# Two hybrid layers and two attention layers on one core: probabilities turned by 32 x 32 blocks, scores as three fp32r products

## The reference, cut to what matters

```python
h = x @ w_in                                   # q, k, v, z for 12 heads of kind a and 12 of kind b, and gates
out_a = dilated_mixture(rope(qa), rope(ka), va)      # with 256 tokens: softmax(q.k/sqrt(128) + log count) @ v
out_b = forgetting_attention(qb, kb, vb, log_f)      # softmax(q.k/sqrt(128) + D_t - D_s), causal, @ v
```

## Time and profile before

| | |
|---|---|
| median of 3 runs | 2801.43 us (2800.37 to 2801.75) |
| the profiled execution | 2799.75 us, its span 2798.0 us |
| TensorE matmul busy | 2757.6 us, 99% |
| VectorE busy | 1817.0 us, 65% |
| ScalarE busy | 1346.3 us, 48% |
| GpSimd busy | 370.9 us, 13% |
| TensorE's granted clock | 0.994 of full |

### The profile page before, as it was taken

How to read it: one execution, slowest core, us unless ns; L and a number is a source line. 1 busy time by engine, 2 the same in 40 slices (tenths; PEclk the granted TensorE clock), 3 DMA queues, 4 the chain that set the end, 5 groups by cost and what they waited for, 6 DMA issues and landing times.

```text
span 2798.0 us, 35964 instructions
## 1 busy us (share of the span) xinstructions
PE 2757.6 (99%) x13157; PEld 2253.2 (81%) x13157; DVE 1817.0 (65%) x2220; ACT 1346.3 (48%) x1765; POOL 370.9 (13%) x653
## 2 busy tenths in 40 slices
PE   8899999999999999999999999999999999999998
PEld 5477887888888888888888888888888888888886
DVE  7889899778657556655555556575565545555565
ACT  3255646556544453544444544444445444445443
POOL 0000010000001223100133100022131011331000
PEclk9999999999999999999999999999999999999999
DMA  9987798865655566566566566565566665665554
GB/s 397 414 311 241 272 342 307 309 222 190 215 194 181 188 201 205 185 220 196 191 202 203 191 196 223 181 195 187 191 203 205 208 199 183 206 206 187 193 213 148
DMA packets 178617, 622.74 MB, mean 223 GB/s; under 512 B 27688, under 2 KB 27984, under 8 KB 173088
## 3 DMA queue, kind: packets, MB, share of 16 engines
q1 hardware_dynamic: 155376, 583.08, 60.3%
q0 software_dynamic: 23088, 37.56, 4.6%
HBM read 599.51 MB, written 2.14 MB: 215 GB/s over the span
## 4 chain that ended last, share of the span: by engine, by line
PE 90%; DMA 4%; DVE 4%; ACT 1%; issue 0%; SPq 0%; DVEq 0%; ACTq 0%
PE acc L860 65%; PE acc L2455 16%; DMA raw<-in_w 2%; DVE wlo L1865 1%; PE psS L839 1%; PE psS L829 1%; DMA scr<-in_w_early 1%; PE psS L2455 1%; PE psS L2421 1%; PE psT L812 1%; PE psT L2378 1%; DMA mraw<-in_w_early 1%; DVE raw L1900 0%; PE psS L2440 0%; PE psT L2340 0%
## 5 line engine op out<-in xcount | busy, mean ns | idle before, releaser
L489 DVE TENSOR_TENSOR wlo<-raw,whi 128x1024 fp32r<-128x1024 f32 x670 | 819.4, 1224 | 783.7 <-ACT whi L372 782.0
L372 ACT ACTIVATE whi<-raw 128x1024 fp32r<-128x1024 f32 x670 | 708.9, 1059 | 980.3 <-PE acc L860 964.4
L860 PE MATMUL acc<-whi,tokens_hi 128*128 128x512 f32 x2304 | 632.3, 395 | 0.5 <-DVE tokens_lo L303 0.3
L860 PE MATMUL acc<-whi,tokens_lo 128*128 128x512 f32 x2304 | 618.2, 389 | 0.0
L860 PE MATMUL acc<-wlo,tokens_hi 128*128 128x512 f32 x2304 | 618.1, 389 | 0.0
L860 PEld LDWEIGHTS acc<-whi,tokens_lo 128*128 128x128 f32 x2304 | 432.4, 188 | 91.5
L860 PEld LDWEIGHTS acc<-wlo,tokens_hi 128*128 128x128 f32 x2304 | 432.4, 188 | 91.0
L860 PEld LDWEIGHTS acc<-whi,tokens_hi 128*128 128x128 f32 x2304 | 425.7, 188 | 85.6 <-DVE tokens_lo L303 0.9
L1564 ACT ACTIVATE whi<-raw 128x1024 fp32r<-128x1024 f32 x160 | 168.7, 1058 | 200.8 <-PE acc L2455 116.2
L1865 DVE TENSOR_TENSOR wlo<-raw,whi 128x1024 fp32r<-128x1024 f32 x160 | 195.3, 1223 | 82.2 <-ACT whi L1564 81.3
L2455 PE MATMUL acc<-whi,tokens_hi 128*128 128x512 f32 x800 | 226.1, 403 | 1.9 <-DVE tokens_lo L1974 1.2
(11 more groups left out here) (355 smaller groups left out, 2434.2 us busy)
## 6 DMA issues: line engine op xcount, KB each, us to landing
raw<-in_w SPq DMA_DIRECT2D x838, 512.0 KB, 4.2
raw<-in_w_late SPq DMA_DIRECT2D x80, 512.0 KB, 5.0
mraw<-in_w SPq DMA_DIRECT2D x64, 512.0 KB, 4.7
mraw<-in_w_late SPq DMA_DIRECT2D x48, 512.0 KB, 4.8
y<-in_w_early SPq DMA_DIRECT2D x12, 1024.0 KB, 15.4
mraw<-in_w_early SPq DMA_DIRECT2D x7, 1024.0 KB, 14.9
scr<-in_w_early SPq DMA_DIRECT2D x7, 1024.0 KB, 14.8
sgl<-in_w_early SPq DMA_DIRECT2D x6, 1024.0 KB, 15.0
```

What stands on the lines that cost most here:

```text
L372: act.activation(whi[:, n % SLOTS, :], raw[:, n % SLOTS, :], ACT.Copy).then_inc(s_hi, 1)
L489: dve.tensor_tensor(wlo[:, n % SLOTS, :], raw[:, n % SLOTS, :], whi[:, n % SLOTS, :].bitcast(F32), ALU.subtract).then_inc(s_lo, 1)
L860: m = pe.matmul(acc[c % 2][:, tb, :], a[:, kk, tb * P:(tb + 1) * P], b[:, n % SLOTS, k * CW:(k + 1) * CW], start=(kk == 0 and q == 0), sto ...
```

## The change

The probabilities no longer pass through TensorE and ScalarE. At r = 35 VectorE turns all three units at once in 32 x 32 blocks into `pb`, which lies in the memory of `qT` and `kT`, and GpSimd moves the blocks to `probT` with 16 transfers of 32 partitions x 12 runs of 32 numbers. The scores become three fp32r products each (`qhi` `khi`, `qlo` `khi`, `qhi` `klo`), all three units in one place at r = 27; the halves are made by ScalarE and VectorE at their steps 27 (q) and 28 (k) and share memory with `stage`, `blocks` and `qkT`. Score unit 2 uses a `psT` bank as a fill. Both value units stand at r = 38. The turned heads move from r = 42 to r = 44. GpSimd's order becomes qT, kT, probT, zT.

```diff
-R_SCORES = 26
-R_BLOCKS = R_SCORES + 16
+R_SCORES = 27
+R_PROB = R_SCORES + 8
+R_BLOCKS = R_SCORES + 17
@@ fills2
-        if 0 <= r - R_SCORES - 5 <= 2:
-            out += [("p", grp, r - R_SCORES - 5)]
+        if r == R_SCORES:
+            out += [("s", grp, 2)]
@@ units2
-        if 0 <= r - R_SCORES <= 2:
-            out += [("s", grp, r - R_SCORES)]
-        if 0 <= r - R_SCORES - 10 <= 1:
-            out += [("o", grp, r - R_SCORES - 10)]
+        if r == R_SCORES:
+            out += [("s", grp, 0), ("s", grp, 1)]
+        if r == R_SCORES + 11:
+            out += [("o", grp, 0), ("o", grp, 1)]
@@ memory
+    stage, qhi = shared("stage", [P, TB, CW], "qhi", [P, HPG, SEQ])
+    qkT, qklo = shared("qkT", [P, 2 * HPG, SEQ], "qklo", [P, 2 * HPG, SEQ])
+    pb = qkT[:].rearrange("p h t -> p (h t)")[:, 0:3 * CW]
+    blocks, khi = shared("blocks", [P, TB, CW], "khi", [P, HPG, SEQ])
@@ gpsimd, regrouped
-                pool.wait_ge(s_blk, 3 * n + i + 1)
-                if grp:
-                    pool.wait_ge(*unit_full(l, ("s", grp - 1, 2)))
+                pool.wait_ge(s_blk, 4 * n + i + 1)
+                if n:
+                    pool.wait_ge(s_pT, MOVED * n)
...
-            pool.wait_ge(s_blk, 3 * n + 3)
+            pool.wait_ge(s_blk, 4 * n + 3)
             if n:
                 pool.wait_ge(s_alo, n)
+            blocks_moved(probT[:].rearrange("p u (k t) -> p (u k) t", t=P), pb.rearrange("p (k t) -> p k t", t=P), s_pT)
+            pool.wait_ge(s_blk, 4 * n + 4)
             blocks_moved(zT, zb, s_zT)
@@ scalar, attention
+                if r in (R_SCORES, R_SCORES + 1):
+                    which = r - R_SCORES
+                    whole, high_part, _, landed = parts[which]
+                    act.wait_ge(landed, MOVED * (NGRP * l + grp + 1))
+                    act.wait_ge(s_blk, 4 * (NGRP * l + grp) + 2)
+                    act.activation(high_part[:], whole[:], ACT.Copy).then_inc(s_qkh, 1)
...
-                if 0 <= r - R_SCORES - 9 <= 2:
-                    u = r - R_SCORES - 9
-                    if u == 0 and NGRP * l + grp:
-                        act.wait_ge(s_alo, NGRP * l + grp)
-                    fill_copy(("p", grp, u), probT[:, u, :])
@@ vector, attention
+                if r in (R_SCORES, R_SCORES + 1):
+                    which = r - R_SCORES
+                    whole, high_part, low_part, _ = parts[which]
+                    dve.wait_ge(s_qkh, 2 * (NGRP * l + grp) + which + 1)
+                    dve.tensor_tensor(low_part[:], whole[:], high_part[:].bitcast(F32), ALU.subtract)\
+                        .then_inc(s_qkl, 1)
...
+                if r == R_PROB:
+                    dve.wait_ge(s_exp, at(l, 3 * NGRP, 3 * grp + 3))
+                    dve.transpose(pb, prob[:].rearrange("p u n -> p (u n)")).then_inc(s_blk, 1)
@@ tensor
+            def scores(name, bank):
+
+                _, grp, u = name
+                pe.wait_ge(s_qkl, 2 * (NGRP * l + grp + 1))
+                w, tb = (P, 0) if u == 0 else (SEQ, 1)
+                for b in range(CW // w):
+                    h = b + max(0, 2 * (u - 1))
+                    for i, (a, k) in enumerate(((qhi, khi), (qlo, khi), (qhi, klo))):
+                        m = pe.matmul(bank[:, b * w:(b + 1) * w], a[:, h, tb * P:(tb + 1) * P], k[:, h, 0:w],
+                                      start=(i == 0), stop=(i == 2))
+                return m
...
-                    pe.wait_ge(s_exp, at(l, 3 * NGRP, 3 * name[1] + name[2] + 1))
-                    for k in range(4):
-                        t = pe.transpose(bank[:, k * P:(k + 1) * P], prob[:, name[2], k * P:(k + 1) * P], ident[:])
+                    t = scores(name, bank)
...
-                    for p in ((0,), (1, 2))[tb]:
-                        pe.wait_ge(*copied(l, ("p", grp, p)))
+                        pe.wait_ge(s_pT, MOVED * (NGRP * l + grp + 1))
```

More of the change, by code:

```diff
@@ L89 @@
 QUADS = P // QUAD
+MOVED = 16 * QUADS * QUADS
 def group_step(c, g):
@@ L166, in sem, with shared @@
         return keep.enter_context(nc.semaphore(name))
+    def shared(name, shape, split_name, split_shape):
+        with nc.sbuf_tensor(name, shape, F32) as tile:
+            pass
+        return tile, sb(split_name, split_shape, F32R)
     ahi = sb("ahi", [P, KT_UP, SEQ], F32R)
@@ L170, in second_block @@
     gb = sb("gb", [P, TB, D])
-    stage = sb("stage", [P, TB, CW])
-    qT = sb("qT", [P, HPG, SEQ])
-    kT = sb("kT", [P, HPG, SEQ])
+    stage, qhi = shared("stage", [P, TB, CW], "qhi", [P, HPG, SEQ])
+    qkT, qklo = shared("qkT", [P, 2 * HPG, SEQ], "qklo", [P, 2 * HPG, SEQ])
+    qT, kT = qkT[:, 0:HPG, :], qkT[:, HPG:, :]
+    qlo, klo = qklo[:, 0:HPG, :], qklo[:, HPG:, :]
     v = sb("v", [P, TB, CW])
@@ L216, in second_block @@
     s_kT = sem("c_kT")
+    s_pT = sem("c_pT")
     s_zT = sem("c_zT")
     s_ahi = sem("c_ahi")
+    s_qkh = sem("c_qkh")
+    s_qkl = sem("c_qkl")
     s_alo = sem("c_alo")
@@ L582, in rope @@
                     if which:
-                        dve.wait_ge(s_blk, 3 * n + 1)
-                        dve.wait_ge(s_qT, 16 * QUADS * QUADS * (n + 1))
+                        dve.wait_ge(s_blk, 4 * n + 1)
+                        dve.wait_ge(s_qT, MOVED * (n + 1))
                     elif n:
-                        dve.wait_ge(s_blk, 3 * n - 1)
+                        dve.wait_ge(s_blk, 4 * n - 1)
                 half = HD // 2
@@ L628, in attention @@
                     name = ("s", grp, u)
-                    bank = UNIT2[name] % 2
+                    if u < 2:
+                        bank, full, free = psS[UNIT2[name] % 2], unit_full(l, name), s_sfree[UNIT2[name] % 2]
+                        read = unit_read(l, name)
+                    else:
+                        bank, full, free = bank_t(name), filled(l, name), s_tfree[FILL2[name] % 2]
+                        read = copied(l, name)
                     n, w = (HPG, P) if u == 0 else (2, SEQ)
@@ L637, in attention @@
                             dve.wait_ge(s_cmask, l + 1)
-                    dve.wait_ge(*unit_full(l, name))
+                    dve.wait_ge(*full)
                     if u == 0 and NGRP * l + grp:
-                        dve.wait_ge(s_zT, 16 * QUADS * QUADS * (NGRP * l + grp))
+                        dve.wait_ge(s_zT, MOVED * (NGRP * l + grp))
                     p = prob[:, u, :].rearrange("p (h s) -> p h s", s=w)
-                    dve.tensor_tensor(p, psS[bank][:].rearrange("p (h s) -> p h s", s=w), m, ALU.add)\
-                        .then_inc(s_sfree[bank], 1)
-                    dve.wait_ge(*unit_read(l, name))
+                    dve.tensor_tensor(p, bank[:].rearrange("p (h s) -> p h s", s=w), m, ALU.add).then_inc(free, 1)
+                    dve.wait_ge(*read)
                     if grp >= 3 and u == 0:
@@ L651, in attention @@
                     link(dve.reciprocal(rden[:], den[:]))
-                if 0 <= r - R_SCORES - 14 <= 1:
-                    tb = r - R_SCORES - 14
+                if 0 <= r - R_SCORES - 15 <= 1:
+                    tb = r - R_SCORES - 15
                     name = ("o", grp, tb)
@@ L820, in unit @@
                 if name[0] == "s":
-                    _, grp, u = name
-                    if u == 0:
-                        pe.wait_ge(s_qT, 16 * QUADS * QUADS * (NGRP * l + grp + 1))
-                        pe.wait_ge(s_kT, 16 * QUADS * QUADS * (NGRP * l + grp + 1))
-                    w, tb = (P, 0) if u == 0 else (SEQ, 1)
-                    for b in range(CW // w):
-                        h = b + max(0, 2 * (u - 1))
-                        out = bank[:, b * w:(b + 1) * w]
-                        m = pe.matmul(out, qT[:, h, tb * P:(tb + 1) * P], kT[:, h, 0:w], start=True, stop=True)
+                    m = scores(name, bank)
                 elif name[0] == "o":
```

24 lines of the change are left out of this document (9 added, 15 removed).

## The result

| | before | after |
|---|---|---|
| median of 4 runs | 2800.9 us (2799.95 to 2801.75) | 2858.2 us (2852.55 to 2861.38) |
| ratio, 95% interval | | 1.0203 [1.0191, 1.0216] |
| span of the profiled execution | 2798.0 us | 2859.7 us |
| TensorE's mean granted clock | 0.994 | 0.987 |

The change makes the kernel 57 us (2.0%) slower. The forecast was 2812 us, slower by 10.6, with a range up to 2838. The sign is right; the time lies outside the range.

A forecast was written before the change was run, and what follows sets the result against it. TensorE, covering 99% of the span, was taken as the bound. From 2801.4 us, -17.5 (transposes) - 0.1 (scores) + 28 (wait for probabilities) = +10.6 gave 2812 us, range 2790 to 2838.

The forecast's parts named there:

- The bound: TensorE covers 99% of the span: work leaving its queue is gained in full, a wait before it lost in full.
- The transposes: TensorE's transposes of the probabilities go: -1.46 us a group, -17.5 us in all.
- The narrow fp32r products: Score matmuls of 128 columns on TensorE: 0.113 us each, set by the weight load, same as for 256 columns.
- the scores: TensorE's score products: 2.72 us a group after against 2.73 before, -0.1 us in all.
- The rivals with 0.227 and 0.057 us: Narrow score products cost as fp32 (0.227 us, 2828 us total, chance 0.2) or columns only (0.057 us, 2804, chance 0.1).
- that of 875 ns an issue: Rival: GpSimd's issue time grows with its runs, the wait is 6 us a group, 2856 us total; chance 0.07.
- The chain from X: Seven steps from the granule behind the scores to landed probabilities: ends X + 29.4 us, TensorE arrives at X + 27.2.
- the seventh: Last step of the probabilities' chain, issue to landing of GpSimd's transfers: 3.9 us, bounds 2.1 and 5.
- The wait for the turned probabilities: TensorE's wait before the value units at step 38: some 2.35 us a group, +28 us over twelve groups.
- The step on k: k's halves ready before TensorE's step 27: 1.7 us to spare, 0.3 in groups 2 and 3, no cost.
- the other moved steps: Halves of q and k on ScalarE and VectorE, and GpSimd's later queues: no cost to TensorE.
- the largest of its terms: The wait on TensorE before the value units for the turned probabilities: +28 us in all.

The follow-up runs named there:

- e6_all_two: Changed kernel with half of the transfers for q, k and probabilities issued by ScalarE's queue, the rest and the heads by GpSimd; 2785.9 us, ratio 0.995.
- e11_all_two_f: e6_all_two with the forget-gate products four granules later; 2783.4 us, ratio 0.9939.
- e8_scores_only: Kernel before the change with only the new fp32r scores and halves at r = 27, probabilities still turned by TensorE; 2800.9 us, ratio 1.0003.
- e12_fewer: Changed kernel with the 16 probability transfers at 32 KB instead of 48 KB, so some values are not the reference's; 2821.7 us, ratio 1.0076.
- e1_warm: Changed kernel with 20 idle transposes of the identity on TensorE ahead of the wait for the turned probabilities; 2846.5 us, ratio 1.017.
- e3_qfirst: Changed kernel with GpSimd moving the next group's q before the turned heads, and the heads split eight granules later; 2852.0 us, ratio 1.0177.
- e2_late: Changed kernel with value units and heads two granules later and forget-gate products four granules later; 2855.1 us, ratio 1.0209.
- e5: Changed kernel with half of the probabilities' 16 transfers issued by ScalarE's queue, half by GpSimd; 2806.5 us, ratio 1.0025.
- e7_fp32: Changed kernel with the scores as single fp32 products without halves, still all at r = 27; 2851.2 us, ratio 1.0183.
- e4_both: Changed kernel with the edits of e2_late and e3_qfirst together; 2817.9 us, ratio 1.0064.

## Why the prediction was right and wrong

**Right.** The bound: what leaves TensorE's queue is gained, a wait in front of it is lost. The transposes gave the forecast 17.5 us or nearly, as soon as nothing else stood in the way: 14.5 us in e6_all_two with 2.3 us of waits left, 17.0 in e11_all_two_f without them. The narrow fp32r products cost 0.11 us (128 columns) and 0.12 (256), where 0.113 was taken between 0.057 and 0.227; the scores are even: 2.80 us a group for 2.73, and e8_scores_only is 0.5 us from the kernel before, where -0.1 was forecast. The rivals with 0.227 and 0.057 us, and that of 875 ns an issue, are out. The Trainium skill's 81 ns a matmul at 128 columns (TensorE: Matmul & The Clock Gate, "Back-to-back issue gap") is not seen in this stream: 926.61 - 926.50 = 0.11 us.

The chain from X = 931.02, the start of granule 28 in the first group's trace, is right up to the last issue. POOL starts at 947.08, X + 16.06 (forecast 16.2), with issues of 616 ns (632), and the last issue starts at 956.18, X + 25.2 (25.5). The block turn takes 1.77 us (1.86). TensorE is at the value units at X + 27.2 as forecast. The other eleven groups have the same offsets within 0.1 us; only the landing differs.

**The step that failed first** is the seventh: "With half as many bytes more each, I take 3.9 us; bounds 2.1 and 5." The last landing takes 4.64 us in the first group, 5.32 in the second and 6.03 in the twelfth. Issue to landing of the first group's batch and of the twelfth's:

```profile
DMA to landing us min/median/max: 2.0/4.2/4.6
...
DMA to landing us min/median/max: 1.9/4.3/6.0
```

The mean of the twelve is 5.12 us: 1.2 over the value taken, and over its upper bound of 5, which 8 of the 12 exceed. I had scaled up the 3.0 to 3.5 us of zT's batch, whose transfers are of 32 KB and ran while the DMA engines were less busy (a share of 0.76 in the ten us from 968.00 before, of 0.93 in those from 947.00 after). That fell short twice. e12_fewer takes 3.96 us in the mean for 32 KB in this very place, so the place alone makes it more than zT's; and from there 48 KB are 29% more. The 1.2 us make 14.6 in 12 groups, less 4 for issues that ended sooner than forecast. So the forecast wait of 2.35 us a group became 38.6 / 12 = 3.2: +10 us.

**A term that was not in the sum** is the granted clock. The part "The wait for the turned probabilities" priced a wait by its length and "a load of 0.19 us to get going". Idle times of 2.6 to 4.0 us are followed, in 7 of 12 groups, by products at 1.2 GHz for some 2 to 5 us: +14 us behind the value waits, and some +10 us behind the scores' waits. e1_warm shows the first to be the clock by filling part of the same wait; in e12_fewer the waits of at most 1.9 us in front of the value products have no such price. The forecast 2.35 us for each wait lies between those cases, so whether the sum would have been short with the right length is not shown. The trace of before had no idle time in the attention stretch, but it did show the fall elsewhere, which I did not read. In its first block, the two rows of TensorE behind a wait of 2.13 and of 2.17 us, and the windows over the four us from there:

```profile
70.33 1.25 PE L2467 MATMUL acc<-raw,zt 128*128 128x512 f32 x2 [2.13 <-ACT zt L1585]
...
86.82 3.70 PE L2467 MATMUL acc<-scr,zt 128*128 128x512 f32 x8 [2.17 <-ACT zt L1585]
...
70.33:74.33 4.00, 4.00 (x6) 1.84 (x7) 3.38 (x4) 0.61 (x1) 3.94 (x8) 0.61 1.01 415
86.82:90.82 4.00, 4.00 (x10) 1.79 (x11) 3.49 (x4) 0.61 (x1) 0.00 (x0) 1.00 1.01 417
```

The clock is 0.61 behind the one and full behind the other. A rival could have been priced from these rows: a granted clock of half for the 2.7 us behind each wait, 12 x 2.7 = 32 us at most.

**The step on k failed in groups 2 and 3 of a layer.** It said: "About half of the delay is caught at VectorE, an estimate; 1.4 us of it reaches k, and 0.3 us of the margin remains." The chain of the second group after:

```profile
996.05 5.16 DMA qkT<-blocks
...
1017.92 5.76 DMA qkT<-blocks
1023.71 1.06 ACT khi L418
1024.80 1.24 DVE qklo L635
...
1026.17 1.53 PE psT L814 x6
```

Measured against TensorE's arrival at the scores (1026.17 - 3.53 = 1022.64 after, 1015.66 + 2.72 = 1018.38 before), q's issues start 35.2 us ahead for 38.6, so 3.4 us later than before; 2.8 were forecast. VectorE's rotation of k then waits 3.47 us for q, and k's issues start 1022.64 - 1009.24 = 13.4 us ahead, where they had 1018.38 - 1001.86 = 16.5. So VectorE catches next to nothing of the delay: 3.1 us of it reach k, not 1.4. The other half is k's landing. I had taken 3.5 us, the slowest of zT's last three; the trace of before had k's own in the second group, which I did not read. Columns: issue to landing, min, median, max. Before:

```profile
DMA to landing us min/median/max: 2.2/3.3/4.0
```

and after:

```profile
DMA to landing us min/median/max: 2.3/5.2/5.8
```

5.76 for 3.5 is 2.3 us more. Together 1.7 + 2.3 = 4.0 us turn the margin of 0.3 into a wait of 3.5 or so. The four waits cost 11.3 us and with the clock 21. That their cause is the heads' transfers in front of q, e3_qfirst shows by taking all four away. Why k's landing grew by 1.8 us against the kernel before, with the same 32 KB and the same issues of 583 ns, is not shown; the DMA engines' share was 0.82 in 1001 to 1011 us before and is 0.87 in 1009 to 1019 us after.

**A miss of 2.3 us**: the forget-gate products, which the value units at r = 38 and VectorE's later step push against each other. The prediction names "the other moved steps" and leaves these out. e11_all_two_f shows them to be worth 2.5 us.

So of the 47 us between forecast and result, 10 are the wait's length, 14 the clock behind it, 21 the scores of four groups, and 2 to 3 the forget gates. That the forecast had the right sign is not to its credit in full: the largest of its terms was right in kind and 10 us short, and effects worth 37 us stood in it at nothing.

**What stays open.** Why the same idle time is followed by a batch at half clock in one group and by a full-speed one in the next (half clock after 3.50 and 2.58 us, not after 3.25 and 2.63 us); no run varied the work ahead of a wait. Why the last landing of the same batch is 4.64 us in one group and 6.03 in another; the weights' own transfers run at the same time, but no run took them away, so that is argued only. And what of the differences between the kernels with waits is chance: the last landings, and behind which of the waits the clock falls, differ from group to group within one execution, and only one execution of each kernel was traced.

## What to carry to other kernels

Price a wait in front of TensorE at its length plus what may follow it at half clock, and look at the granted clock of the stretch behind it before taking a wait of 2 to 4 us for cheap. Here the waits' own length was 53 us and the clock behind them 23 more. When a step is moved onto a queue, lay out all batches of that queue over a whole period (here four batches of 16 issues, 9.2 to 9.7 us each) with the landing of the last of a batch under load, since shifting one later (e2_late) moved the wait to the next batch, and putting one first (e3_qfirst) took one wait away and left the other. Where issues are the long part of a chain, a second queue (e5, e6) shortens it without any order to find.

## What the runs showed of the hardware

- In front of the value products, the kernel after, e3_qfirst, e7_fp32 and e1_warm have 37 idle times of 2.45 to 4.59 us. Behind 30 of them TensorE's clock was at its lower level for part or all of the batch (0.50 to 0.69 granted over it); behind 7 it was full. Behind the 20 of 0.4 to 1.9 us there (e12_fewer, e1_warm) it was always full. But the scores of the change's third group, after a wait of only 1.44 us, took 3.87 us for 2.77: the products up to 1128.68 still stand 0.11 to 0.12 us apart and those from there on 0.21, so no length of a wait can be called safe. And the second group's scores in e1_warm, after 2.73 us, ran at full clock.
- In the slow second group of e4_both a product of 128 columns stands 0.21 us from the next, twice the 0.11 us at full clock.
- An fp32r product of 128 columns (0.11 us) is hardly cheaper than one of 256 (0.12 us), while an fp32 product of 128 columns costs 0.23 and one of 256 costs 0.43. So whether three narrow passes pay depends on the width; in this mix they cost 2.80 us a group against 2.63.
- A batch of 16 transfers between places in on-chip memory spreads in its landing: of the first group's batch to `probT` the quickest lands 2.0 us after its issue, the median 4.2, the last 4.6. From group to group the last takes 4.64 to 6.03 us.
- The issue of such a transfer takes 0.65 us on ScalarE's queue in e6_all_two (8 from 946.86, done 5.47 us on), about the same as GpSimd's 0.62 us (8 from 947.12, done 4.88 us on). Two queues help by working side by side; neither issues faster.
